# Weighing every second gathered row on VectorE instead of TensorE, with a ring of ten buffers

## The chip, the cores and the metric

The kernel runs on one core of one Trainium2 chip. The metric is the device time of one execution in microseconds (us). Before the change it is 3411.38 us, the median of three executions (3409.58 to 3421.29). The profile is of one further execution, whose own time was 3418.78 us.

## The reference, cut to what matters

Two transformer blocks run one after the other on 512 tokens of width 1024, all in float32. The first has a mixture-of-experts layer, the second ends in a layer that looks up single-neuron experts by product keys. The change is in that last layer alone:

```python
def peer_ffn(h, w_query, keys1, keys2, expert_u, expert_v):
    q = (hf @ w_query).reshape(t, PEER_HEADS, 2, PEER_HALF)        # 8 heads, 2 x 128
    s1 = jnp.einsum('thc,hnc->thn', q[:, :, 0], keys1)             # 128 keys each
    s2 = jnp.einsum('thc,hnc->thn', q[:, :, 1], keys2)
    ...                                                            # top 16 of 16 x 16 sums: idx, gate
    def block(args):
        hb, ib, gb = args
        act = jax.nn.gelu(jnp.einsum('thkd,td->thk', expert_u[ib], hb), approximate=False)
        return jnp.einsum('thk,thkd->td', gb * act, expert_v[ib])
```

Each token has 8 heads with 16 picks, 128 in all. For every pick a row `u` of 1024 and a row `v` of 1024 numbers are fetched; the dot product of `u` with the token goes through a gelu and times a gate becomes the pick's weight; the 128 rows `v` are summed with their weights. The block's output is that sum plus the residual, normalised by its root mean square.

## The kernel before, in words

The whole program is one launch in stages. The last stage is the function `peer`, which fills the last 40% of the execution. The 512 tokens lie in four tiles of 128, one token to a partition. The table `peer_uv` holds `u` and `v` of an expert side by side, 2048 numbers or 8 KB.

*Rows and ring.* A "row" in what follows is one indirect DMA of GpSimd (line 1833): for pick n of a tile it fetches 128 entries of `peer_uv`, one for each token, 1 MB in all, into slot n % RING of `ring`. RING is 11. There are 4 x 128 = 512 rows. GpSimd issues them in order; row n waits until row n - 11 is spent (line 1832).

*Batches and groups.* Two rows make a batch (256 batches), eight batches a group: the 16 picks of one head for one tile (32 groups). Groups alternate between tiles 0 and 1 for the first 16 groups, then between tiles 2 and 3.

*VectorE* runs in the order that the loop at line 2066 writes out: for batch b `products(b)` (two dot products of `u` with the token, line 2040, each behind the wait for its row), then `mixing(b - 1)` (weight = gelu times gate, two numbers for each token, line 2048). In the middle of every group, after batch 4 of 8, stands `retrieve(g + 2)` (lines 2005 to 2031): the top-16 search that finds the picks for the group after next. It runs for all groups but the last two, so 30 times in the loop. Before the loop stand `retrieve(0)` and `retrieve(1)`.

*ScalarE* computes the gelu of each batch (line 1941) and, in `diagonals`, for each row a 128x128 matrix with the weights on its diagonal (line 1948).

*TensorE* multiplies each row's diagonal matrix by the row's `v` half, in two calls of 512 columns that add into the tile's two PSUM banks (line 1907), and after each row raises `spent`. In float32 a call is two recorded passes, so a row has four. Between batches it also does what is left of the queries and scores for the first ten groups.

*End of a tile.* In groups 15, 16 and 31, at batches 2 and 3 of the group, ScalarE squares a finished tile's sum (`squares`, line 1956) and VectorE normalises it (`finish`, lines 2053 to 2058); the last tile is finished after the loop. SyncE stores it.

Of the kernel before, what the change touches and what calls it, by code (L numbers as in the profile page):

```python
# [18 lines left out]
ACT = mybir.ActivationFunctionType  # L19
ALU = mybir.AluOpType  # L20
AX = mybir.AxisListType

P = 128
D = 1024
# [4 lines left out]
NT = SEQ // P  # L29
# [18 lines left out]
HG_W = HG_H * HG_D  # L48
KH = HG_W // P
PEER_H, NKEYS, TOPK = 8, 128, 16  # L50
RING = 11
LEVELS = (32, 16, 8, 4, 2, 1)


# [1706 lines left out]
def peer(core, A, hn, out):  # L1761

    nc, ps, ident = core.nc, core.psum, core.ident
# [4 lines left out]
    DIAGS = 4  # L1768
    with core.stage("peer") as st:
# [14 lines left out]
        pick = st.sb("pick", [P, NT, PICKS], U32)  # L1784
        gate, dots = st.sb("gate", [P, NT, PICKS]), st.sb("dots", [P, NT, PICKS])
        acts, mix = st.sb("acts", [P, DIAGS, BATCH]), st.sb("mix", [P, DIAGS, BATCH])
        diag = st.sb("diag", [P, DIAGS, BATCH, P])
        stat = st.sb("stat", [P, NT, 4])
        hr = core.w.rows[:].rearrange("p (i b) c -> p i (b c)", b=2)
        gain = core.w.tiles[:, 0].rearrange("p k c -> p (k c)")  # L1790
        res = core.w.tiles[:, 1].rearrange("p k c -> p (k c)")
        (loaded, own, q_out, s_ps, s_out, r_ps, r_out, picked, e_in, e_out, dotted, gelued, mixed, diagonal, spent,
         squared, meaned, rooted, done, saved, gain_in) = (
            st.sem(n) for n in ("ld", "own", "qo", "sp", "so", "rp", "ro", "pick", "ei", "eo", "dot", "gelu", "mix",
                                "diag", "spent", "sq", "mean", "root", "done", "saved", "gain"))
        landed = [st.sem(f"row{n}") for n in range(RING)]
        w_ready, w_used, turns = core.w.ready, core.w.summed, core.w.turns

# [2 lines left out]

        def head_of(g):
            return g % (2 * H) // 2

        def place(b):
            g = b // PER
            return tile_of(g), head_of(g) * K + b % PER * BATCH

        with nc.Block() as block:
# [14 lines left out]
            @block.gpsimd  # L1824
            def _(pool):
                for n in range(NT * PICKS):
                    g, slot = n // K, n % RING
                    i, j = tile_of(g), head_of(g) * K + n % K
                    if n % K == 0:
                        pool.wait_ge(picked, g + 1)  # L1830
                    if n >= RING:
                        pool.wait_ge(spent, n - RING + 1)
                    pool.indirect_dma_start(out=ring[:, slot], out_offset=None, in_=A["peer_uv"],  # L1833
                                            in_offset=bass.IndirectOffsetOnAxis(ap=pick[:, i, j:j + 1], axis=0)
                                            ).then_inc(landed[slot], 16)

            @block.tensor
            def _(pe):
                def query(h, s):
                    m = 2 * h + s  # L1840
                    pe.wait_ge(w_ready[m % U], 16 * (turns + m // U + 1))
                    if h >= 1:
                        pe.wait_ge(q_out, 2 * (h - 1) + s + 1)
                    for k in range(KD):
                        last = nc.tensor.matmul(ps[:, 4 + s], core.w.tiles[:, m % U, k], hn[:, k], start=k == 0, stop=k == KD - 1)  # L1845
                    last.then_inc(w_used[m % U], 1)
# [19 lines left out]
                def residual(i):  # L1866
                    for k in range(KD):
                        nc.tensor.matmul(ps[:, 2 * i + k // 4, (k % 4) * P:(k % 4 + 1) * P],
                                         core.h[:, k, META + i * P:META + (i + 1) * P], ident[:],
                                         start=k % 4 == 0, stop=False, skip_group_check=True)  # L1870

                query(0, 0)
                query(0, 1)
                rows(0, 0)
# [11 lines left out]
                for b in range(BATCHES):  # L1886
                    i, j = place(b)
                    g, at = b // PER, b % PER
                    if g < 10 and at == 0:
                        query(3 + g // 2, g % 2)  # L1890
                    if g < 10 and g % 2 == 1 and at == PER // 2:
                        scores(3 + g // 2)
                    if g == 11 and at == 0:
                        pe.wait_ge(q_out, 2 * H)
                        rows(2, 4)
                    if g == 12 and at == 0:
                        pe.wait_ge(s_out, 2 * H)
                        rows(3, 6)
                    if g in (14, 15) and at == 0:
                        pe.wait_ge(r_out, 2 * NT)  # L1900
                        residual(g - 12)
                    pe.wait_ge(diagonal, BATCH * (b + 1))
                    for x in range(BATCH):
                        slot = (b * BATCH + x) % RING
                        end = j + x == PICKS - 1
                        for c in range(2):
                            last = nc.tensor.matmul(ps[:, 2 * i + c], diag[:, b % DIAGS, x], ring[:, slot, D + 512 * c:D + 512 * (c + 1)],  # L1907
                                                    start=False, stop=end, skip_group_check=True)
                        last.then_inc(spent, 1)

            @block.scalar
            def _(act):
# [30 lines left out]
                def diagonals(b):  # L1943
                    act.wait_ge(mixed, b + 1)
                    if b >= DIAGS:
                        act.wait_ge(spent, BATCH * (b - DIAGS + 1))
                    for x in range(BATCH):
                        act.activation(diag[:, b % DIAGS, x], ident[:], ACT.Copy, scale=mix[:, b % DIAGS, x:x + 1]).then_inc(diagonal, 1)  # L1948

                def squares(i):  # L1950
                    act.wait_ge(spent, PICKS * (2 * (i // 2) + 2) - (K if i % 2 == 0 else 0))
                    if i == 0:
                        act.wait_ge(gain_in, 16)
                    if i >= 1:
                        act.wait_ge(saved, 16 * i)
                    act.activation(res.rearrange("p (b c) -> p b c", b=2),
                                   ps[:, 2 * i:2 * i + 2], ACT.Square, accum_out=stat[:, i, 0:1]).then_inc(squared, 1)
                    act.wait_ge(meaned, i + 1)
                    act.activation(stat[:, i, 3:4], stat[:, i, 2:3], ACT.Sqrt).then_inc(rooted, 1)
# [33 lines left out]
            def _(dve):  # L1993
# [49 lines left out]
                def mixing(b):  # L2043
                    i, j = place(b)
                    dve.wait_ge(gelued, b + 1)
                    if b >= DIAGS:
                        dve.wait_ge(diagonal, BATCH * (b - DIAGS + 1))
                    dve.tensor_tensor(mix[:, b % DIAGS], acts[:, b % DIAGS], gate[:, i, j:j + BATCH],
                                      ALU.mult).then_inc(mixed, 1)

                def finish(i):
                    dve.wait_ge(squared, i + 1)
# [13 lines left out]
                for b in range(BATCHES):  # L2066
                    g, at = b // PER, b % PER
                    products(b)
                    if b >= 1:
                        mixing(b - 1)  # L2070
                    if at == PER // 2 and g + 2 < GROUPS:
                        retrieve(g + 2)
                    if g in (15, 16, 31) and at == 3:
                        finish({15: 0, 16: 1, 31: 2}[g])
                mixing(BATCHES - 1)
                finish(NT - 1)


# [129 lines left out]
```

## Time and profile before

| | |
|---|---|
| median of three executions | 3411.38 us (3409.58 to 3421.29) |
| the profiled execution's own time | 3418.78 us |
| its span | 3417.0 us |
| first and last issue of a row (line 1833) | 2043.6 and 3386.1 us |
| last dot product of a row starts (line 2040) | 3400.5 us |
| TensorE, VectorE, ScalarE, GpSimd busy over the span | 80%, 39%, 16%, 21% |
| mean granted clock of TensorE | 0.916 |

Times in the profile count from the start of the span. An engine is busy while an instruction of it executes; where it was idle, the profile names what released it. A row of a timeline gives start, duration and engine, then line, operation, output<-inputs and how many instructions were merged, and in brackets how long the engine sat idle before it and what ended that. VectorE is DVE, ScalarE is ACT, GpSimd is POOL and TensorE is PE there.

### The profile page before, as it was taken

Reading aid. Unit: us, or ns where it says so; the run is one execution under the profiler, and the core shown is the slowest. Engines: PE = TensorE matmul, PEld = TensorE weight load, DVE = VectorE, ACT = ScalarE, POOL = GpSimd, SP = SyncE. Lnnn points to the kernel's source line nnn. Section 1 sums busy time; section 2 is a strip of 40 time slices with the busy share of each in tenths; the row PEclk is TensorE's granted clock in tenths of the full one; section 3 lists DMA queues with packets and bytes.
Section 4 is the critical chain, followed back from the end, with each engine's and each line's share of the span. In section 5 each row is a group of like instructions: output and inputs, shape, how many; then the busy total and the mean of one; then the engine's idle time right before and its main releaser. Section 6 shows DMA issues by size and latency. Waiting matters only on the chain. (4 is left out here: it accounts for less than half of the span.)

```text
span 3417.0 us, 25695 instructions
## 1 busy us (share of the span) xinstructions
PE 2738.9 (80%) x9100; PEld 1266.1 (37%) x9100; DVE 1342.2 (39%) x3184; ACT 543.6 (16%) x1320; POOL 724.8 (21%) x624
## 2 busy tenths in 40 slices
PE   6999497777888787479899989888877777777777
PEld 4654333332333333234454444333433323323332
DVE  2151400000000000235320236767777777676674
ACT  2031100000000000021102012222222222222222
POOL 0000100000000000002420003444444444444442
PEclk9999699999999999689999999999988888888889
DMA  3003399999999999310112229999999999999998
GB/s 134 25 19 146 110 378 426 426 427 426 423 421 422 407 419 417 125 52 32 50 41 76 74 80 405 412 401 411 396 400 406 399 402 393 394 396 404 393 411 336
DMA packets 135119, 1017.95 MB, mean 298 GB/s; under 512 B 26624, under 2 KB 27344, under 8 KB 44368
## 3 DMA queue, kind: packets, MB, share of 16 engines
q0 software_dynamic: 83200, 545.33, 39.4%
q1 hardware_dynamic: 51792, 470.98, 33.8%
q8 instruction: 73, 1.20, 0.1%
q14 instruction: 54, 0.44, 0.0%
HBM read 1020.38 MB, written 21.02 MB: 305 GB/s over the span
## 5 line engine op out<-in xcount | busy, mean ns | idle before, releaser
L1907 PE MATMUL psum<-peer_ring,peer_diag 128*128 128x512 f32 x2048 | 970.1, 633 | 289.1 <-ACT peer_diag L1948 289.0
L1833 POOL DMA_INDIRECT peer_ring<-in_peer_uv,peer_pick x512 | 573.8, 1121 | 1063.5 <-PE psum L1907 739.3
L2040 DVE CUSTOM_DVE_ANT_0 peer_ring<-peer_ring,sb_rows 128x1024 f32<-128x1024 f32 x512 | 618.2, 1224 | 370.2 <-DMA peer_ring<-in_peer_uv,peer_pick 368.8
L1907 PEld LDWEIGHTS psum<-peer_ring,peer_diag 128*128 128x128 f32 x2048 | 408.4, 203 | 843.2 <-issue 483.2
L1089 PE MATMUL psum<-ffn1w_w,ffn_y 128*64 128x512 f32 x2048 | 487.4, 631 | 146.4 <-DMA ffn1w_w<-in_w_up 98.3
L1133 DVE TENSOR_TENSOR ffn_y<-psum,ffn_y 128x512 f32<-128x512 f32 x32 | 22.1, 692 | 883.7 <-ACT ffn_y L1117 883.7
L1089 PEld LDWEIGHTS psum<-ffn1w_w,ffn_y 128*64 128x64 f32 x2048 | 177.3, 145 | 455.2 <-issue 453.5
L1423 PE MATMUL psum<-mix_xn,sb_tiles 128*128 128x512 f32 x640 | 288.1, 612 | 14.7 <-DMA mix_heads<-in_head_pairs 14.7
L1110 PE MATMUL psum<-ffn1w_w,moe_hT 128*64 128x512 f32 x1024 | 230.0, 601 | 37.0 <-DVE moe_hT L1138 29.0
L1168 POOL DMA_INDIRECT expert_rows<-sb_tiles,ffn_block_tok x32 | 32.7, 1021 | 901.2 <-ACT sb_tiles L1123 874.7
L1941 ACT ACTIVATE peer_acts<-peer_dots 128x2 f32<-128x2 f32 x256 | 52.0, 203 | 880.1 <-DVE peer_dots L2040 880.0
L1423 PEld LDWEIGHTS psum<-mix_xn,sb_tiles 128*128 128x128 f32 x640 | 124.8, 197 | 171.5 <-issue 155.3
L1948 ACT ACTIVATE peer_diag<-sb_ident,peer_mix 128x128 f32<-128x128 f32 x512 | 173.5, 386 | 0.3
L1110 PEld LDWEIGHTS psum<-ffn1w_w,moe_hT 128*64 128x64 f32 x1024 | 85.3, 138 | 159.5 <-issue 159.5
L1845 PE MATMUL psum<-ffn_hn,sb_tiles 128*128 128x512 f32 x256 | 115.3, 604 | 11.4 <-PEq L144 10.5
L1117 ACT ACTIVATE ffn_y<-psum 128x512 f32<-128x512 f32 x32 | 19.1, 597 | 605.5 <-PE psum L1089 605.5
L412 PE MATMUL psum<-mix_xn,sb_tiles 128*128 128x264 f32 x384 | 91.5, 400 | 13.9 <-PEq L144 11.0
L1037 POOL DMA_INDIRECT slot_tokens<-ffn1r_tok,ffn_slots x8 | 8.0, 996 | 401.9 <-DVEq L1021 399.8
L1630 POOL TENSOR_TENSOR mix_K<-mix_z,mix_F 128x2048 f32<-128x2048 f32 x6 | 35.6, 5938 | 239.0 <-DVEq L1706 151.6
L412 PEld LDWEIGHTS psum<-mix_xn,sb_tiles 128*128 128x128 f32 x384 | 74.8, 197 | 29.9 <-issue 16.4
L1123 ACT ACTIVATE sb_tiles<-psum 128x512 f32<-128x512 f32 x64 | 34.7, 595 | 319.0 <-PE psum L1110 319.0
L1845 PEld LDWEIGHTS psum<-ffn_hn,sb_tiles 128*128 128x128 f32 x256 | 49.3, 194 | 73.8 <-issue 73.8
(351 smaller groups left out, 2112.1 us busy)
## 6 DMA issues: line engine op xcount, KB each, us to landing
ffn1w_w<-in_w_gate SPq DMA_DIRECT2D x64, 2048.0 KB, 28.9
ffn1w_w<-in_w_up SPq DMA_DIRECT2D x64, 2048.0 KB, 28.7
ffn1w_w<-in_w_down SPq DMA_DIRECT2D x64, 2048.0 KB, 29.9
sb_tiles<-in_w_in2b SPq DMA_DIRECT2D x28, 512.0 KB, 3.5
sb_tiles<-in_w_out SPq DMA_DIRECT2D x16, 512.0 KB, 3.5
sb_tiles<-in_w_query SPq DMA_DIRECT2D x16, 512.0 KB, 5.6
peer_ring<-in_peer_uv,peer_pick POOLq DMA_INDIRECT x512, 11.6
sb_tiles<-in_w_in SPq DMA_DIRECT2D x12, 512.0 KB, 3.5
```

Source lines behind the costliest of these rows:

```text
L412: last = nc.tensor.matmul(ps[:, bank(name) + half, 0:HALF], w_tile[:, n % U, k], xn[:, k, c], start=k == 0, stop=k == KD - 1)
L1089: last = nc.tensor.matmul(ps[r, bank], xT[:, u, k, r], weights(slots[half], k, F, 0, F), start=k == 0, stop=k == KD - 1)
L1110: last = nc.tensor.matmul(ps[r, 6 + b], hT[:, k, r], weights(slots[half], k, D, b * 512, 512), start=k == 0, stop=k == KE - 1)
L1123: act.activation(yo[:, u, b * 512:(b + 1) * 512], ps[:, 6 + b], ACT.Copy).then_inc(yo_ready, 1)
L1423: last = nc.tensor.matmul(ps[:, bank_of(n)], w_tile[:, n % U, c], xn[:, c], start=c == 0, stop=c == KD - 1)
L1630: pool.tensor_tensor(K[:, n % 2], k, F[:, n % 2], ALU.mult).then_inc(kl, 1)
L1833: pool.indirect_dma_start(out=ring[:, slot], out_offset=None, in_=A["peer_uv"], in_offset=bass.IndirectOffsetOnAxis(ap=pick[:, i, j:j + 1] ...
L1845: last = nc.tensor.matmul(ps[:, 4 + s], core.w.tiles[:, m % U, k], hn[:, k], start=k == 0, stop=k == KD - 1)
L1907: last = nc.tensor.matmul(ps[:, 2 * i + c], diag[:, b % DIAGS, x], ring[:, slot, D + 512 * c:D + 512 * (c + 1)], start=False, stop=end, sk ...
L1941: act.activation(acts[:, b % DIAGS], dots[:, i, j:j + BATCH], ACT.Gelu).then_inc(gelued, 1)
L1948: act.activation(diag[:, b % DIAGS, x], ident[:], ACT.Copy, scale=mix[:, b % DIAGS, x:x + 1]).then_inc(diagonal, 1)
L2040: dve.tensor_tensor_reduce(ring[:, n % RING, 0:D], ring[:, n % RING, 0:D], hr[:, i], 1.0, 0.0, ALU.mult, ALU.add, dots[:, i, j + x:j + x + ...
```

## The change

The first row of each batch goes the old way. The second row (odd n) is no longer given a diagonal matrix or multiplied on TensorE. VectorE multiplies its `v` half by the weight and adds it to a running sum of the tile in SBUF, `summed_rows`, in one instruction over 1024 columns; the first of a tile only multiplies. This is `weigh(b - 2)`, placed behind `mixing(b - 1)` and ahead of `retrieve`. When a tile is complete, TensorE adds its `summed_rows` to the tile's PSUM by two calls with the identity matrix (`fold`), and `squares` waits for that. The ring has ten slots, so that a slot always holds rows of the same parity; the issue of row n waits for `spent` or for `weighed` by that parity.

```diff
-RING = 11
+RING = 10
...
-        diag = st.sb("diag", [P, DIAGS, BATCH, P])
+        diag = st.sb("diag", [P, DIAGS, P])
+        summed_rows = st.sb("summed_rows", [P, 2, D])
...
+        def batches_of(i):
+            return NT * PICKS // BATCH // 2 * (i // 2 + 1) - (PER if i % 2 == 0 else 0)
...
                     if n >= RING:
-                        pool.wait_ge(spent, n - RING + 1)
+                        pool.wait_ge(weighed if (n - RING) % 2 else spent, (n - RING) // 2 + 1)
...
+                def fold(i):
+                    pe.wait_ge(weighed, batches_of(i))
+                    for c in range(2):
+                        last = nc.tensor.matmul(ps[:, 2 * i + c], ident[:], summed_rows[:, i % 2, 512 * c:512 * (c + 1)],
+                                                start=False, stop=True, skip_group_check=True)
+                    last.then_inc(folded, 1)
...
-                    pe.wait_ge(diagonal, BATCH * (b + 1))
-                    for x in range(BATCH):
-                        slot = (b * BATCH + x) % RING
-                        end = j + x == PICKS - 1
-                        for c in range(2):
-                            last = nc.tensor.matmul(ps[:, 2 * i + c], diag[:, b % DIAGS, x], ring[:, slot, D + 512 * c:D + 512 * (c + 1)],
-                                                    start=False, stop=end, skip_group_check=True)
-                        last.then_inc(spent, 1)
+                    pe.wait_ge(diagonal, b + 1)
+                    slot = b * BATCH % RING
+                    for c in range(2):
+                        last = nc.tensor.matmul(ps[:, 2 * i + c], diag[:, b % DIAGS], ring[:, slot, D + 512 * c:D + 512 * (c + 1)],
+                                                start=False, stop=False, skip_group_check=True)
+                    last.then_inc(spent, 1)
+                    if g in (15, 16, 31) and at == 1:
+                        fold({15: 0, 16: 1, 31: 2}[g])
+                fold(NT - 1)
...
                     if b >= DIAGS:
-                        act.wait_ge(spent, BATCH * (b - DIAGS + 1))
-                    for x in range(BATCH):
-                        act.activation(diag[:, b % DIAGS, x], ident[:], ACT.Copy, scale=mix[:, b % DIAGS, x:x + 1]).then_inc(diagonal, 1)
+                        act.wait_ge(spent, b - DIAGS + 1)
+                    act.activation(diag[:, b % DIAGS], ident[:], ACT.Copy, scale=mix[:, b % DIAGS, 0:1]).then_inc(diagonal, 1)
...
                 def squares(i):
-                    act.wait_ge(spent, PICKS * (2 * (i // 2) + 2) - (K if i % 2 == 0 else 0))
+                    act.wait_ge(folded, i + 1)
...
+                def weigh(b):
+                    i, j = place(b)
+                    row = ring[:, (b * BATCH + 1) % RING, D:2 * D]
+                    dve.wait_ge(mixed, b + 1)
+                    if j == 0:
+                        if i >= 2:
+                            dve.wait_ge(folded, i - 1)
+                        dve.tensor_scalar(summed_rows[:, i % 2], row, mix[:, b % DIAGS, 1:2], None, ALU.mult).then_inc(weighed, 1)
+                    else:
+                        dve.wait_ge(weighed, b)
+                        dve.scalar_tensor_tensor(out=summed_rows[:, i % 2], in0=row, scalar=mix[:, b % DIAGS, 1:2],
+                                                 in1=summed_rows[:, i % 2], op0=ALU.mult, op1=ALU.add).then_inc(weighed, 1)
...
                     products(b)
                     if b >= 1:
                         mixing(b - 1)
+                    if b >= 2:
+                        weigh(b - 2)
                     if at == PER // 2 and g + 2 < GROUPS:
                         retrieve(g + 2)
...
                 mixing(BATCHES - 1)
+                weigh(BATCHES - 2)
+                weigh(BATCHES - 1)
                 finish(NT - 1)
```

## Rows read from the trace of the kernel before

**Rows 1.** The page's second part: the span in 40 equal slices.
```profile
DMA  3003399999999999310112229999999999999998
GB/s 134 25 19 146 110 378 426 426 427 426 423 421 422 407 419 417 125 52 32 50 41 76 74 80 405 412 401 411 396 400 406 399 402 393 394 396 404 393 411 336
```
**Rows 2.** Stretch, length; busy PE, PEld, DVE, ACT, POOL; clock, DMA share, GB/s.
```profile
2056.00:3402.00 1346.00, 1055.96 (x2359) 456.68 (x2357) 931.58 (x2491) 314.60 (x931) 564.31 (x502) 0.90 0.99 402
```
**Rows 3.** Groups by line from 1900 us on.
```profile
L1907 PE MATMUL psum<-peer_ring,peer_diag 128*128 128x512 f32 x2048 | 970.1, 633 | 289.1 <-ACT peer_diag L1948 289.0
L2040 DVE CUSTOM_DVE_ANT_0 peer_ring<-peer_ring,sb_rows 128x1024 f32<-128x1024 f32 x512 | 618.2, 1224 | 370.2 <-DMA peer_ring<-in_peer_uv,peer_pick 368.8 <-DVE sb_tiles L2058 0.4
L1833 POOL DMA_INDIRECT peer_ring<-in_peer_uv,peer_pick x512 | 573.8, 1121 | 1063.5 <-PE psum L1907 739.3 <-DVE peer_pick L2028 293.9 <-issue 30.3
```
**Rows 4.** The chain of waits in order of time: the first and 30th such TensorE burst.
```profile
2094.05 15.19 PE psum L1907 x28
...
3318.76 20.69 PE psum L1907 x44
```
**Rows 5.** Timeline of VectorE around one retrieve.
```profile
2798.68 1.23 DVE L2040 CUSTOM_DVE_ANT_0 peer_ring<-peer_ring,sb_rows 128x1024 f32<-128x1024 f32 x1 [1.26 <-DMA peer_ring<-in_peer_uv,peer_pick]
...
2799.90 0.29 DVE L1999 MAX8 peer_val<-peer_far 128x8 f32<-128x128 f32 x1
...
2810.80 1.23 DVE L2040 CUSTOM_DVE_ANT_0 peer_ring<-peer_ring,sb_rows 128x1024 f32<-128x1024 f32 x1
...
2813.17 1.22 DVE L2040 CUSTOM_DVE_ANT_0 peer_ring<-peer_ring,sb_rows 128x1024 f32<-128x1024 f32 x1
...
2821.12 1.23 DVE L2040 CUSTOM_DVE_ANT_0 peer_ring<-peer_ring,sb_rows 128x1024 f32<-128x1024 f32 x1 [0.77 <-DMA peer_ring<-in_peer_uv,peer_pick]
2824.62 1.23 DVE L2040 CUSTOM_DVE_ANT_0 peer_ring<-peer_ring,sb_rows 128x1024 f32<-128x1024 f32 x1 [2.27 <-DMA peer_ring<-in_peer_uv,peer_pick]
...
2828.13 1.22 DVE L2040 CUSTOM_DVE_ANT_0 peer_ring<-peer_ring,sb_rows 128x1024 f32<-128x1024 f32 x1 [2.20 <-DMA peer_ring<-in_peer_uv,peer_pick]
...
2838.09 1.23 DVE L2040 CUSTOM_DVE_ANT_0 peer_ring<-peer_ring,sb_rows 128x1024 f32<-128x1024 f32 x1 [1.19 <-DMA peer_ring<-in_peer_uv,peer_pick]
2840.59 1.22 DVE L2040 CUSTOM_DVE_ANT_0 peer_ring<-peer_ring,sb_rows 128x1024 f32<-128x1024 f32 x1 [1.27 <-DMA peer_ring<-in_peer_uv,peer_pick]
```
**Rows 6.** Timeline of GpSimd and of TensorE around the same retrieve.
```profile
2804.76 0.94 POOL L1833 DMA_INDIRECT peer_ring<-in_peer_uv,peer_pick  x1 [0.78 <-PE psum L1907]
2818.11 1.82 POOL L1833 DMA_INDIRECT peer_ring<-in_peer_uv,peer_pick  x1 [12.41 <-PE psum L1907]
2821.02 0.94 POOL L1833 DMA_INDIRECT peer_ring<-in_peer_uv,peer_pick  x1 [1.09 <-PE psum L1907]
...
2814.06 16.13 PE L1907 MATMUL psum<-peer_ring,peer_diag 128*128 128x512 f32 x30 [9.57 <-ACT peer_diag L1948]
```
**Rows 7.** Timeline: an issue that starts just behind a dot product.
```profile
2663.96 1.23 DVE L2040 CUSTOM_DVE_ANT_0 peer_ring<-peer_ring,sb_rows 128x1024 f32<-128x1024 f32 x1 [1.26 <-DMA peer_ring<-in_peer_uv,peer_pick]
...
2664.03 1.96 POOL L1833 DMA_INDIRECT peer_ring<-in_peer_uv,peer_pick  x1 [0.53 <-PE psum L1907]
```
**Rows 8.** Groups by line, shapes apart: the same operation as the added one.
```profile
L171 DVE SCALAR_TENSOR_TENSOR ffn_hn<-sb_h,sb_vec,n_rs 128x512 f32<-128x512 f32 x8 | 5.4, 748 | 0.7 <-ACT n_rs L150 0.7
...
L1300 DVE SCALAR_TENSOR_TENSOR comb_g<-comb_g,ffn_gates 128x1024 f32<-128x1024 f32 x4 | 5.1, 1284 | 0.1
```
**Rows 9.** Timeline of ScalarE and VectorE where tile 1 is finished.
```profile
2703.47 1.00 ACT L1956 ACTIVATE sb_tiles<-psum 128x1024 f32<-128x1024 f32 x1
...
2708.38 1.41 DVE L2058 SCALAR_TENSOR_TENSOR sb_tiles<-psum,peer_stat,sb_tiles 128x512 f32<-128x512 f32 x2 [0.33 <-ACT peer_stat L1959]
...
2710.54 1.23 DVE L2040 CUSTOM_DVE_ANT_0 peer_ring<-peer_ring,sb_rows 128x1024 f32<-128x1024 f32 x1 [0.75 <-DMA peer_ring<-in_peer_uv,peer_pick]
```
**Rows 10.** Timeline of the end: the last dot product, and the last tile's squares.
```profile
3400.52 1.23 DVE L2040 CUSTOM_DVE_ANT_0 peer_ring<-peer_ring,sb_rows 128x1024 f32<-128x1024 f32 x1 [1.24 <-DMA peer_ring<-in_peer_uv,peer_pick]
...
3409.80 1.02 ACT L1956 ACTIVATE sb_tiles<-psum 128x1024 f32<-128x1024 f32 x1 [6.64 <-PE psum L1907]
```

More of the change, by code:

```diff
@@ L1791, in peer @@
         res = core.w.tiles[:, 1].rearrange("p k c -> p (k c)")
-        (loaded, own, q_out, s_ps, s_out, r_ps, r_out, picked, e_in, e_out, dotted, gelued, mixed, diagonal, spent,
+        (loaded, own, q_out, s_ps, s_out, r_ps, r_out, picked, e_in, e_out, dotted, gelued, mixed, diagonal, spent, weighed, folded,
          squared, meaned, rooted, done, saved, gain_in) = (
             st.sem(n) for n in ("ld", "own", "qo", "sp", "so", "rp", "ro", "pick", "ei", "eo", "dot", "gelu", "mix",
-                                "diag", "spent", "sq", "mean", "root", "done", "saved", "gain"))
+                                "diag", "spent", "weighed", "folded", "sq", "mean", "root", "done", "saved", "gain"))
         landed = [st.sem(f"row{n}") for n in range(RING)]
@@ L2046, in mixing @@
                     if b >= DIAGS:
-                        dve.wait_ge(diagonal, BATCH * (b - DIAGS + 1))
+                        dve.wait_ge(diagonal, b - DIAGS + 1)
                     dve.tensor_tensor(mix[:, b % DIAGS], acts[:, b % DIAGS], gate[:, i, j:j + BATCH],
                                       ALU.mult).then_inc(mixed, 1)
+                def weigh(b):
[10 more added lines that the diff above has]
+                                                 in1=summed_rows[:, i % 2], op0=ALU.mult, op1=ALU.add).then_inc(weighed, 1)
                 def finish(i):
```

## The prediction

> **What bounds the kernel now.** I read the page's slices first, to place the stage. In the last 17 slices, which are the gather stage, the DMA share stands at nine tenths or more, at 393 to 412 GB/s almost throughout [rows 1]. The view by stretches says it more sharply: from 2056 to 3402 us the DMA share is 0.99, while TensorE is busy 1056 of 1346 us, VectorE 932, GpSimd 564 and ScalarE 315 [rows 2]. Then the groups by line, for who waits for whom: VectorE sat idle 369 us before its dot products for the DMA of the row, TensorE 289 us for the diagonals behind them, and GpSimd 739 us for TensorE to free a slot [rows 3]. The last looks like a case against TensorE, but a ring behind a full queue is always full: that wait costs only what leaves the queue short of rows. So the stage is bound by the DMAs; 512 rows of 1.05 MB.
>
> The chain of waits has one burst of TensorE in each of the 30 groups that hold a `retrieve`; first and 30th begin 1224.7 us apart, so a group of 16 rows takes 1224.7/29 = 42.2 us [rows 4]. Undisturbed rows land 2.50 us apart (2838.09 to 2840.59), 40.0 us a group [rows 5]. The missing 2.2 us are lost after `retrieve`, and there the change acts. The timelines show it. Put t = 0 where the last dot product before it starts, at 2798.68. `retrieve` starts at 1.2 and occupies VectorE for 10.9; the next dot product starts at 12.1 [rows 5]. With 11 slots, nine rows are on order meanwhile: batches up to the one before are freed by TensorE early in the `retrieve`, the last by the issue at 2804.76 [rows 6]. The next batch's mixing must come before TensorE goes on: it restarts at 15.4, and its first row (late, after 9.6 us of idleness) frees a slot at 19.4 (2818.11), where GpSimd had waited 12.4 us [rows 6]. That issue takes 1.82 us, to 21.2, and its row lands at 25.9, 4.7 after the issue's end; the ninth had landed at 22.4. So 25.9 is 1.0 later than a full queue would give (24.9), and the row behind it comes 3.5 instead of 2.5 after it [rows 5, 6].
>
> **The change, part by part.**
>
> *Removed from TensorE and ScalarE:* half of 2048 passes (485 of 970 us busy) and 256 of 512 diagonals [rows 3]. Worth nothing by itself: both engines are covered by the DMAs. Four `fold`s add 16 passes, at most 10 us by the mean of 633 ns, covered but at the end. TensorE will be idle oftener; its half-rate start costs nothing as long as a row's 4 us [rows 6] fits in a batch's 5.
>
> *Added to VectorE:* 252 multiply-adds over 128x1024 from SBUF, and 4 plain multiplies. The trace has that very form once, at 1284 ns (two 512-wide ones would be 1496) [rows 8]. A dot product of 1224 ns [rows 3] follows the last after 1.15, so I take 1.21 us of pace, from 1.15 (nothing above a dot product) to 1.5 as bounds. A group of VectorE is now 8 x 2.37 (2810.80 to 2813.17) + 10.9 = 29.9 us [rows 5]; it becomes 29.9 + 8 x 1.21 = 39.5 of the 42.2. It still fits, but its slack falls from 12.3 us to 2.7.
>
> *Moved: when slots come free.* This is what I expect to decide. An odd row is freed only by `weigh(b - 2)`, one iteration later than the mixing, and `weigh` shares VectorE's queue with `retrieve`. At the start of `retrieve`, behind batch b, the weighs have got to b - 2. The odd row of batch b - 1 is thus held until the next iteration, and issues are in order. With ten slots, rows up to 2b + 8 are on order: seven instead of nine, 17.5 us of transfer instead of 22.5. One of the two lost rows is the ring's eleventh slot, the other the held odd row. The time line becomes: `weigh` 1.2, so `retrieve` from 2.4 to 13.3; two dot products and mixing to 15.7; `weigh(b - 1)` to 17.0; GpSimd some 0.3 later at 17.3. That is 2.1 earlier than the 19.4 of now, since it doesn't wait for TensorE.
>
> *The issue itself.* The next dot product has just started by then, and issues that start behind one are long: 1.96 us when it had begun 0.07 earlier, 0.94 when free [rows 6, 7]. So it ends at 19.1 and the row lands at 19.1 + 4.7 = 23.8. That is the row that a full queue gives at 8 x 2.5 = 20.0. The gap grows from 1.0 to 3.8 us, so +2.8 for each `retrieve`.
>
> On this the Trainium skill has a rule (SBUF — State Buffer, "Who interferes with whom"): a VectorE instruction with two SBUF inputs contends with a GpSimd instruction that reads SBUF, and the one that issued first keeps the shared port. The 1.96 us issue agrees. The added instruction is of that sort too, so by this rule it also speaks against the change; without it the issue would take 0.94 and the sum would be some 27 us smaller.
>
> *A shallow queue after the gap.* Today most issues behind the gap are short, and the queue refills as fast as TensorE frees slots. Then they fall where VectorE runs two-input instructions without a break, so each may take up to 1.96 us [rows 7] and the pause between two, hardly less than the 2.5 in which a row lands. The row after a gap takes 3.5 instead of 2.5 today [rows 5]; up to two more may do so. Bounds 0 to +1.8 a group; I take +0.4, near the lower end, since VectorE frees slots in backlog at 3.6 us for two.
>
> *Sum for a `retrieve`:* +2.8 + 0.4 = +3.2 us. Bounds: +1.9 with a short issue; +4.6 with the whole shallow-queue loss; a pace of 1.15 or 1.5 changes two weighs, -0.1 or +0.6. Thirty times: 96 us (54 to 156).
>
> *Beginning.* Before the loop's first `retrieve` the first weighs are themselves in backlog: +2.8 once.
>
> *Finishing tiles.* `squares` of tiles 0 and 1 had nothing to wait for at 2703.47; VectorE's normalising then ended at 2709.8, 0.8 before the next row was in [rows 9]. It will wait for a batch's row and the fold, eight passes: 4.3 us at 28 passes in 15.19 [rows 4], 8 at the slow start's 4.05 a row. Between the squares' end at 2704.5 and the normalising at 2708.38 lie 3.9 us, and 0.8 behind it, so a later `retrieve` costs 0 to 3.3 us, twice; I take 3 in all.
>
> *End.* Now 9.3 us pass from the last dot product (3400.52) to the last squares (3409.80), mostly TensorE's last rows [rows 10]. Then: dot product 1.2, three weighs 3.6, fold 2.2 to 4, so 7.0 to 8.8. Gain 0.5 to 2.3; I take 2, since TensorE has had half the rows.
>
> *Total:* 96 + 3 + 3 - 2 = +100 us. On the profiled execution's own 3418.8 us (span 3417.0) that is 3519; that execution lies 7.4 above the median, so I forecast 3411 + 100 = **3511 us**.
>
> **The rivals.**
>
> *Faster: the late restart was the loss.* GpSimd's long wait after `retrieve` is for TensorE, and the change frees every other slot without it. Were seven rows on order enough to bridge the earlier restart, the 2.2 us lost in each group would vanish: 30 x -2.2 = -66, and 3411 - 66 + 4 = 3349 us. For it: the restart is 2.1 earlier, and the slow first rows of TensorE are off half the slots. Against: the lost cover is 5.0 us. It decides only if rows issued at 17.3 land before 20, in 2.7 us, where the trace's fastest issue to landing was 6.3.
>
> *No change: the transfers hide it anyway.* The 5.0 us lost and 2.1 won come out even if the present loss is mostly not the ring's but of the chip's memory. Today some landings are late with rows on order. If such a loss took up the gap, the time would be 3411 + 4 = 3415. Against: the landing at 25.9 follows its issue by the usual 4.7.
>
> *VectorE becomes the bound.* Its group reaches the forecast's 45.4 us when a weigh costs 1.9, and if an issue that starts first held up VectorE for 0.94, sixteen times a group, it would be 39.5 + 15 = 54.5: +12.3 x 30, 3780 us. A weigh of 2.4 (twice a dot product) gives 29.9 + 19.6 = 49.5, +7.3 a group, 3630 us. Against: issues at 2818.11 ran beside dot products that kept their 1.15 us.
>
> By the skill's rule above the hold-up can go that way as well; no row here shows VectorE's pace broken.
>
> **How the numbers follow.** The forecast has 76%, and of itself runs from 3411 + 54 + 0 = 3465 to 3411 + 156 + 8 = 3575. VectorE as the bound has 7% (3575 up), no change 7%, faster 10%. The range is 3440 to 3590: the forecast's own with the neighbourhood of both edges; some 2 in 10 lie outside. A measurement of this kernel tells 0.5%, 17 us, from no change. Slower by more: 76 + 7 = 83%; within: 7%; faster: 10%.
>
> **What would show it.** Right: in the trace after, GpSimd's first issue after `retrieve` released by VectorE's weigh at about 17.3 and long; its row at 23.8 and eighth in line, with seven dot products without a wait before it; a group of 45.4 us; DMA share of the stage down to about 0.92; VectorE busy some 88%; multiply-adds of 1.28 us. Wrong in size: several rows 3.5 apart after the gap. Wrong altogether: groups of 40 to 42 us with the share at 0.99, or VectorE without waits for rows at all.

## Result: 2.4% slower, and the profile after

The change makes the kernel slower: 3500.5 us in the median of four executions (3497.5 to 3504.5) against 3416.3 us of the kernel before (four executions on the same chip). The ratio is 1.0242, with a 95% interval of 1.0216 to 1.0268. The forecast was 3511 us, with a range of 3440 to 3590; 3500.5 lies 10 below it. Part of that nearness is luck: as an increase the forecast said +100 us and the medians say +84, and 5 of the 16 us between them are made up by a kernel before that took 3416.3 us here and 3411.4 in the executions the forecast started from.

The same views as before. First the stretch of the gather stage (length; busy time of the engines; granted clock, DMA share, GB/s), which answers to [rows 2], then the groups by line that answer to [rows 3] and [rows 8] (from 2043 us on, so without the first eight issues).

```profile
2056.00:3480.00 1424.00, 749.61 (x1327) 274.96 (x1326) 1219.14 (x2734) 238.05 (x671) 652.39 (x502) 0.77 0.92 376
```

```profile
L1916 PE MATMUL psum<-peer_ring,peer_diag 128*128 128x512 f32 x1024 | 663.7, 791 | 675.9 <-ACT peer_diag L1959 675.8
L1837 POOL DMA_INDIRECT peer_ring<-in_peer_uv,peer_pick x504 | 654.3, 1298 | 773.8 <-DVE peer_summed_rows L2072 439.2 <-PE psum L1916 224.7 <-issue 104.6
L2051 DVE CUSTOM_DVE_ANT_0 peer_ring<-peer_ring,sb_rows 128x1024 f32<-128x1024 f32 x512 | 615.1, 1222 | 164.4 <-DMA peer_ring<-in_peer_uv,peer_pick 162.2 <-DVE sb_tiles L2082 0.6
L2072 DVE SCALAR_TENSOR_TENSOR peer_summed_rows<-peer_ring,peer_mix,peer_summed_rows 128x1024 f32<-128x1024 f32 x252 | 322.0, 1278 | 0.1
```

The DMA share of the stage fell from 0.99 to 0.92, the figure that the forecast named. VectorE is busy 1219 of 1424 us, 86% (some 88% in the forecast). TensorE lost half its passes but only 306 of 970 us of busy time: the mean pass grew from 633 to 791 ns, since its granted clock fell from 0.90 to 0.77 of 2.4 GHz over the stage. It now waits for the diagonals before most batches, 676 us in all. The multiply-add takes 1278 ns.

Then one `retrieve` of the kernel after, first on VectorE, then on GpSimd and TensorE. It answers to [rows 5, 6]; t = 0 is again the start of the last dot product ahead of it, 2842.46.

```profile
2842.46 1.23 DVE L2051 CUSTOM_DVE_ANT_0 peer_ring<-peer_ring,sb_rows 128x1024 f32<-128x1024 f32 x1 [1.27 <-DMA peer_ring<-in_peer_uv,peer_pick]
...
2843.68 1.28 DVE L2072 SCALAR_TENSOR_TENSOR peer_summed_rows<-peer_ring,peer_mix,peer_summed_rows 128x1024 f32<-128x1024 f32 x1
...
2855.78 1.23 DVE L2051 CUSTOM_DVE_ANT_0 peer_ring<-peer_ring,sb_rows 128x1024 f32<-128x1024 f32 x1
...
2858.15 1.28 DVE L2072 SCALAR_TENSOR_TENSOR peer_summed_rows<-peer_ring,peer_mix,peer_summed_rows 128x1024 f32<-128x1024 f32 x1
2859.35 1.22 DVE L2051 CUSTOM_DVE_ANT_0 peer_ring<-peer_ring,sb_rows 128x1024 f32<-128x1024 f32 x1
...
2871.17 1.22 DVE L2051 CUSTOM_DVE_ANT_0 peer_ring<-peer_ring,sb_rows 128x1024 f32<-128x1024 f32 x1
...
2874.42 1.23 DVE L2051 CUSTOM_DVE_ANT_0 peer_ring<-peer_ring,sb_rows 128x1024 f32<-128x1024 f32 x1 [0.76 <-DMA peer_ring<-in_peer_uv,peer_pick]
```

```profile
2859.70 1.68 POOL L1837 DMA_INDIRECT peer_ring<-in_peer_uv,peer_pick  x1 [11.73 <-DVE peer_summed_rows L2072]
2862.80 1.00 POOL L1837 DMA_INDIRECT peer_ring<-in_peer_uv,peer_pick  x1 [1.42 <-PE psum L1916]
2864.11 1.97 POOL L1837 DMA_INDIRECT peer_ring<-in_peer_uv,peer_pick  x1 [0.30 <-issue]
2866.39 0.97 POOL L1837 DMA_INDIRECT peer_ring<-in_peer_uv,peer_pick  x1 [0.30 <-issue]
...
2858.75 6.09 PE L1916 MATMUL psum<-peer_ring,peer_diag 128*128 128x512 f32 x8 [12.49 <-ACT peer_diag L1959]
```

Weigh at 1.2, next dot product at 13.3, `weigh(b - 1)` from 15.7, and GpSimd released by it at 17.2 with a long issue (1.68 us) to 18.9: each within 0.2 us of the forecast's time line. The release stands at 17.2 in 28 of the 30 groups. One thing is different. VectorE doesn't come to wait for the row issued then. It has so much work that it runs ten dot products without a wait, to 2871.17; only the eleventh, at 32.0, waits for its row. The first dot products that show the empty queue come three rows later than I wrote.

That the queue does stand empty can be read from the DMA engines. These are the four emptiest microseconds around the `retrieve` shown, in the kernel after (15.5 to 19.5 us behind t = 0) and, below, in the kernel before (19.3 to 23.3). The columns are those of [rows 2]; the DMA share is the last but one:

```profile
2858.00:2862.00 4.00, 3.25 (x4) 1.17 (x4) 4.00 (x10) 0.74 (x4) 1.68 (x1) 0.50 0.15 61
2818.00:2822.00 4.00, 4.00 (x8) 1.56 (x7) 3.23 (x6) 1.52 (x6) 2.75 (x2) 0.74 0.42 107
```

The trace also has the semaphore updates with which a row's parts are reported, 16 for a row; the row has landed with the last of them. Over the 27 groups in which no tile is finished, the eighth row lands 23.4 us behind t = 0 in the median (forecast 23.8) and 5.9 behind the seventh. With a full queue it is 2.5, and in the kernel before the tenth row lands 3.2 behind the ninth. So the gap stands where the forecast put it and has nearly its size.

### The profile page after: what moved, and what is told of

Read it like the earlier page. It is cut to its first block and busy times, and to the rows that moved or that the text cites. A ratio compares the mean times of both kernels' runs of the same rounds, so it can differ in the third digit from the quotient of the medians.

```text
span 3495.7 us, 23933 instructions
## 1 busy us (share of the span) xinstructions
PE 2444.0 (70%) x8092; PEld 1089.2 (31%) x8092; DVE 1638.2 (47%) x3440; ACT 469.1 (13%) x1064; POOL 812.9 (23%) x624
## 5 line engine op out<-in xcount | busy, mean ns | idle before, releaser
L1916 PE MATMUL psum<-peer_ring,peer_diag 128*128 128x512 f32 x1024 | 663.7, 791 | 675.9 <-ACT peer_diag L1959 675.8
L1837 POOL DMA_INDIRECT peer_ring<-in_peer_uv,peer_pick x512 | 661.9, 1293 | 1069.8 <-DVE peer_summed_rows L2072 439.2
L1089 PE MATMUL psum<-ffn1w_w,ffn_y 128*64 128x512 f32 x2048 | 496.9, 642 | 134.4 <-DMA ffn1w_w<-in_w_up 99.0
L1916 PEld LDWEIGHTS psum<-peer_ring,peer_diag 128*128 128x128 f32 x1024 | 224.4, 241 | 1102.9 <-ACT peer_diag L1959 914.9
L2072 DVE SCALAR_TENSOR_TENSOR peer_summed_rows<-peer_ring,peer_mix,peer_summed_rows 128x1024 f32<-128x1024 f32 x252 | 322.0, 1278 | 0.1
L1959 ACT ACTIVATE peer_diag<-sb_ident,peer_mix 128x128 f32<-128x128 f32 x256 | 98.8, 386 | 1.0 <-DVE peer_mix L2059 0.8
```

The lines of the kernel that those rows point to most:

```text
L1089: last = nc.tensor.matmul(ps[r, bank], xT[:, u, k, r], weights(slots[half], k, F, 0, F), start=k == 0, stop=k == KD - 1)
L1916: last = nc.tensor.matmul(ps[:, 2 * i + c], diag[:, b % DIAGS], ring[:, slot, D + 512 * c:D + 512 * (c + 1)], start=False, stop=False, ski ...
L1959: act.activation(diag[:, b % DIAGS], ident[:], ACT.Copy, scale=mix[:, b % DIAGS, 0:1]).then_inc(diagonal, 1)
L2072: dve.scalar_tensor_tensor(out=summed_rows[:, i % 2], in0=row, scalar=mix[:, b % DIAGS, 1:2], in1=summed_rows[:, i % 2], op0=ALU.mult, op1 ...
```

## Experiments

All are read by the same measure beside their time: the mean length of a group of 16 rows over 29 groups, from the start of the tenth dot product of each group to that of the next group's. It is 42.24 us before and 45.20 after.

### 1. The eleventh slot alone

```diff
--- the kernel before
-RING = 11
+RING = 10
```

> The kernel before with a ring of ten slots instead of eleven, nothing else. Theory (what counts is how many rows are on order while retrieve occupies VectorE, against when the first slot comes free behind it): eight rows on order instead of nine, restart unchanged at 19.4, so the row issued then still lands at 25.9 but is the ninth, not the tenth: +2.5 us in each of 30 groups, +75 us, 3416 to 3491 us, group 44.7 us. Rival (the slot is not scarce, VectorE's added work or the odd row's late release is the whole loss): under +10 us.

Measured: 3490.2 us, ratio to before 1.0213 (1.0191 to 1.0234), group 44.89 us. One slot less costs 2.65 us a group, nearly all that the whole change does. Its timelines:

```profile
2836.75 1.23 DVE L2040 CUSTOM_DVE_ANT_0 peer_ring<-peer_ring,sb_rows 128x1024 f32<-128x1024 f32 x1 [1.26 <-DMA peer_ring<-in_peer_uv,peer_pick]
...
2857.11 1.22 DVE L2040 CUSTOM_DVE_ANT_0 peer_ring<-peer_ring,sb_rows 128x1024 f32<-128x1024 f32 x1
2862.59 1.22 DVE L2040 CUSTOM_DVE_ANT_0 peer_ring<-peer_ring,sb_rows 128x1024 f32<-128x1024 f32 x1 [4.18 <-DMA peer_ring<-in_peer_uv,peer_pick]
...
2842.92 0.93 POOL L1833 DMA_INDIRECT peer_ring<-in_peer_uv,peer_pick  x1 [0.31 <-PE psum L1907]
2856.02 1.98 POOL L1833 DMA_INDIRECT peer_ring<-in_peer_uv,peer_pick  x1 [12.17 <-PE psum L1907]
```

The release is where it was (19.3), the row issued then lands at 25.8 as before, but it is the ninth and not the tenth: VectorE waits 4.2 us for it. The rival is out.

### 2. VectorE's added instruction alone

The kernel before, ring of eleven, with a multiply-add of the same shape at the same place; it reads the token's row and leads nowhere. (`sc2`, `cand2` and `hit` share a buffer to make room.)

```diff
+                    dve.scalar_tensor_tensor(out=spare_sum[:], in0=hr[:, i], scalar=mix[:, b % DIAGS, 1:2],
+                                             in1=spare_sum[:], op0=ALU.mult, op1=ALU.add).then_inc(weighed, 1)
...
                         mixing(b - 1)
+                    if b >= 2:
+                        weigh(b - 2)
```

> The kernel before (ring of eleven, all rows on TensorE) with the added multiply-add of VectorE at the same place in its order, but reading the token's row instead of the gathered one and leading nowhere: VectorE's time and port use alone (two scratch tiles share a buffer to make room). Theory: retrieve starts 1.2 us later and with it the mixing that restarts TensorE: +1.2 us a group, +36 us, some 3452 us, no more since 39.5 us of VectorE still fit in a group. Rival (VectorE's load or its hold on GpSimd's issues is the loss): +85 us or more, 3500.

Measured: 3451.8 us, 1.0098 (1.0074 to 1.0123), group 43.28 us, +1.04. The slot that TensorE frees behind `retrieve` comes free at 20.6 instead of 19.4 in the trace, and that is all: VectorE's 39.5 us fit. The rival is out.

### 3. The kernel after with eleven slots

```diff
--- the kernel after
-RING = 10
+RING = 11
```

(With the shared buffer and `KEPT`, the number of score tiles held, 3 instead of 4, since the eleventh slot and the 8 KB of sums don't fit otherwise.)

> The kernel after with a ring of eleven (two scratch tiles share a buffer and one kept score tile less, to make room). Theory: eight rows on order instead of seven during retrieve, release at 17.3 unchanged: -2.5 us a group, about -75 us, 3425 us, group 42.2. Rival (VectorE's own order is what paces the group now): under -20 us, above 3480.

Measured: 3420.4 us, 1.0008 (0.9996 to 1.0020) to the kernel before, group 42.40 us. The slot takes back 2.80 of the 2.96 us that the change cost. With eleven slots each the two kernels are the same within measurement. `KEPT` 3 was not run by itself; the first six groups are longer than in the kernel before (43.6 against 42.6 us in the mean) and the other 23 are not (42.1 against 42.2).

### 4. The odd row free one iteration sooner

```diff
--- the kernel after
-                    if b >= 2:
-                        weigh(b - 2)
+                    if b >= 1:
+                        weigh(b - 1)
```

> The kernel after, with each weigh directly behind its own batch's mixing instead of one iteration later, ring of ten. The odd row of batch b-1 is free before retrieve, so eight rows are on order instead of seven. Theory: the next row then waits for TensorE's even row of batch b, whose mixing comes at 15.7 and whose slow first passes end at about 19.9; with its issue it lands at about 26.4, where the same row lands in the kernel after anyway. So within 15 us of 3500. Rival (the held odd row is one of the two that are missing and costs its 2.5 us): 3425 us.

Measured: 3519.6 us, 1.0304 (1.0282 to 1.0326), group 45.52 us: 19 us slower than the kernel after, 4 outside what I expected, and on the other side from the rival. VectorE and GpSimd behind a `retrieve` (t = 0 at 2855.55):

```profile
2869.00 1.23 DVE L2051 CUSTOM_DVE_ANT_0 peer_ring<-peer_ring,sb_rows 128x1024 f32<-128x1024 f32 x1
2870.15 1.22 DVE L2051 CUSTOM_DVE_ANT_0 peer_ring<-peer_ring,sb_rows 128x1024 f32<-128x1024 f32 x1
2871.49 1.28 DVE L2072 SCALAR_TENSOR_TENSOR peer_summed_rows<-peer_ring,peer_mix,peer_summed_rows 128x1024 f32<-128x1024 f32 x1
2872.69 1.22 DVE L2051 CUSTOM_DVE_ANT_0 peer_ring<-peer_ring,sb_rows 128x1024 f32<-128x1024 f32 x1
...
2875.63 1.64 POOL L1837 DMA_INDIRECT peer_ring<-in_peer_uv,peer_pick  x1 [11.64 <-PE psum L1916]
2877.57 1.98 POOL L1837 DMA_INDIRECT peer_ring<-in_peer_uv,peer_pick  x1 [0.30 <-issue]
```

There is now one row more on order (+2.5 us of cover), but the first release is TensorE's even row, at 20.1 here and 20.45 in most groups, 3.2 later than the weigh's 17.2. The row issued then is the ninth, and it lands at 26.3 in the median; the ninth row of the kernel after, one behind its gap, lands at 26.0. So the theory held, and the row held by the lag was no loss that comes back by freeing it: the next slot in order is TensorE's, and it comes no sooner. A batch in backlog also takes 3.69 us instead of 3.56, as the weigh must wait for the mixing right ahead of it. Only part of the 19 us is the gather stage's: from the first issue to the end of the span it is 9.9 us longer than in the kernel after (0.32 a group), and between the two profiled executions, 17.8 us apart, the other 7.9 lie ahead of the stage, where the code is the same.

### 5 to 7. `retrieve` in three parts

```diff
-                def retrieve(g):
+                def search(g):          # top 16 of both halves
...
+                def combine(g):         # top 16 of the sums, up to e_in
...
+                def pick_rows(g):       # the rest
...
-                    if at == PER // 2 and g + 2 < GROUPS:
-                        retrieve(g + 2)
+                    if at in (2, 4, 6) and g + 2 < GROUPS:
+                        (search, combine, pick_rows)[at // 2 - 1](g + 2)
```

The kernel before with it:

> The kernel before, with retrieve cut into three parts (3.4, 3.1 and 4.3 us) behind batches 2, 4 and 6 of the group instead of one of 10.9 behind batch 4. Theory: nine rows on order outlast every part, so the 2.2 us lost in each group go: group 40.0 to 40.3, -55 to -66 us, 3355 us. Rival (the 2.2 us are the memory's own late landings): within 10 us of 3417.

The kernel after with it:

> The kernel after with the same cut, ring of ten. Theory: the gap behind retrieve goes here too, and what remains is VectorE's 39.5 us a group against 40.0 of transfers: group 40.0 to 41.5, 3360 to 3405 us, DMA share of the stage 0.97 or more. Rival (so little slack makes VectorE the bound, with its long issues): above 3430.

The kernel before with it and ten slots:

> The kernel before with the cut and a ring of ten. Theory: the eleventh slot was worth 75 us only because of the long retrieve; with short parts it is worth under 10 us: 3355 to 3365 us. Rival (a slot is worth 2.5 us a group whatever VectorE's order): 3430.

| `retrieve` in three parts | us | ratio to before | group, us | one piece |
|---|---|---|---|---|
| before, 11 slots | 3377.0 | 0.9899 (0.9882 to 0.9915) | 40.89 | 42.24 |
| before, 10 slots | 3383.1 | 0.9909 (0.9892 to 0.9925) | 41.08 | 44.89 |
| after, 10 slots | 3383.7 | 0.9916 (0.9899 to 0.9932) | 41.09 | 45.20 |

Both kernels before are some 20 us above what I expected, the kernel after is in its range. The slot that was worth 73 us is worth 6, within the intervals. The change, which cost 84 us as it was made, costs 7, hardly more than can be told. So the long `retrieve` is what makes slots count. The kernel before with the cut beats both kernels of this study, by 1.0% and 3.5%. Its timeline around the first part, and the stretch from 2100 to 3300 us of it:

```profile
2798.84 1.23 DVE L2050 CUSTOM_DVE_ANT_0 peer_ring<-peer_ring,sb_rows 128x1024 f32<-128x1024 f32 x1 [1.26 <-DMA peer_ring<-in_peer_uv,peer_pick]
2800.06 0.29 DVE L1999 MAX8 peer_val<-peer_far 128x8 f32<-128x128 f32 x1
...
2803.46 1.22 DVE L2050 CUSTOM_DVE_ANT_0 peer_ring<-peer_ring,sb_rows 128x1024 f32<-128x1024 f32 x1
2804.61 1.22 DVE L2050 CUSTOM_DVE_ANT_0 peer_ring<-peer_ring,sb_rows 128x1024 f32<-128x1024 f32 x1
2806.32 1.23 DVE L2050 CUSTOM_DVE_ANT_0 peer_ring<-peer_ring,sb_rows 128x1024 f32<-128x1024 f32 x1 [0.41 <-DMA peer_ring<-in_peer_uv,peer_pick]
```

```profile
2100.00:3300.00 1200.00, 972.43 (x2147) 405.83 (x2146) 872.12 (x2342) 287.41 (x854) 538.32 (x470) 0.95 1.01 416
```

Two rows of backlog, and the third finds VectorE waiting for it again. The share is 1.01, so the queue doesn't run dry, and yet a group takes 40.9 us in the mean, not the 40.0 that I had set as the floor. The first six groups, in which TensorE also has queries and scores to do, take 41.6; the later ones mostly 39.9 or 40.9. The timeline of VectorE shows what makes the difference, in four dot products of which each had to wait for its row:

```profile
3032.55 1.22 DVE L2050 CUSTOM_DVE_ANT_0 peer_ring<-peer_ring,sb_rows 128x1024 f32<-128x1024 f32 x1 [0.76 <-DMA peer_ring<-in_peer_uv,peer_pick]
3035.04 1.23 DVE L2050 CUSTOM_DVE_ANT_0 peer_ring<-peer_ring,sb_rows 128x1024 f32<-128x1024 f32 x1 [1.19 <-DMA peer_ring<-in_peer_uv,peer_pick]
3038.49 1.23 DVE L2050 CUSTOM_DVE_ANT_0 peer_ring<-peer_ring,sb_rows 128x1024 f32<-128x1024 f32 x1 [2.22 <-DMA peer_ring<-in_peer_uv,peer_pick]
3040.99 1.22 DVE L2050 CUSTOM_DVE_ANT_0 peer_ring<-peer_ring,sb_rows 128x1024 f32<-128x1024 f32 x1 [1.19 <-DMA peer_ring<-in_peer_uv,peer_pick]
```

One row comes 3.45 us behind the last instead of 2.5. By the semaphore updates this happens about once in 22 rows from the eighth group on, once in 18 to 21 in the kernel after with the cut, and few rows are late otherwise; once in 22 makes 0.7 us a group. What delays that row isn't shown. The theory had the mechanism and 20 us too much of it.

### 8. Relief of TensorE alone

```diff
--- the kernel before
-                        for c in range(2):
+                        wide = 512 if x == 0 or end else 64
+                        for c in range(2 if wide == 512 else 1):
```

> The kernel before (ring of eleven), with TensorE's work on odd rows cut to 64 of their 1024 columns (the sum lacks the others), VectorE's order and the slots' release unchanged: the relief of TensorE alone. Theory (TensorE is covered by the transfers, and the slot that counts behind retrieve is an even row's): within 10 us of 3414. Rival (TensorE's slow passes behind retrieve cost the group part of its 2.2 us): -20 to -40 us.

Measured: 3413.4 us, 1.0000 (0.9985 to 1.0014), group 42.39 us. Nearly half of TensorE's work in the stage is worth nothing, though TensorE was busy 1056 of 1346 us of it (786 of 1339 now) and GpSimd waited 739 us for it. One thing this run can't tell: the row that frees the first slot behind `retrieve` is an even one, which it leaves whole, and its slot still comes free at 19.4. Experiment 2 shows that this moment counts: 1.2 us later cost 1.04 us a group. A TensorE faster there was not tried.

### 9. The same time on VectorE with one input from SBUF

```diff
--- the kernel of experiment 2
-                    dve.scalar_tensor_tensor(out=spare_sum[:], in0=hr[:, i], ..., in1=spare_sum[:], op0=ALU.mult, op1=ALU.add)
+                    dve.tensor_reduce(spare_sum[:], hr[:, i], AX.X, ALU.add)
```

> The kernel extra_op with the added multiply-add replaced by a sum over the token's row, an instruction of nearly the same length that reads one SBUF tensor instead of two. Theory by this case's rows (an issue that starts behind a two-input instruction waits for its end): issues behind the sum take 0.94 us again, mean issue down from 1.254 to about 1.12 us; the time follows only where the first issue behind retrieve gets shorter, 0 to 0.9 us a group: 3452 down to 3425 at most. Rival (issue length plays no part in the 1.2 us a group): within 5 us of 3452.

Measured: 3446.3 us, 1.0089 (1.0066 to 1.0112), group 43.16 us; mean issue 1.162 us against 1.254 with the multiply-add. First an issue behind the multiply-add of experiment 2, then one behind the sum:

```profile
2405.99 1.28 DVE L2060 SCALAR_TENSOR_TENSOR peer_spare_sum<-sb_rows,peer_mix,peer_spare_sum 128x1024 f32<-128x1024 f32 x1
...
2406.09 1.99 POOL L1835 DMA_INDIRECT peer_ring<-in_peer_uv,peer_pick  x1 [0.43 <-PE psum L1909]
```

```profile
2444.69 1.21 DVE L2057 TENSOR_REDUCE peer_spare_sum<-sb_rows 128x1 f32<-128x1024 f32 x1
...
2445.00 0.94 POOL L1835 DMA_INDIRECT peer_ring<-in_peer_uv,peer_pick  x1 [0.65 <-PE psum L1909]
```

Counted over the stage, the issues that start with 0.5 us or more of the other instruction still to run: 42 behind the multiply-add take 1.66 us in the mean, 62 behind the sum 0.94, as much as with VectorE idle. What holds an issue is the second input from SBUF. Here the Trainium skill (SBUF — State Buffer, "Who interferes with whom") says just this, and the trace agrees. In time it is little: the two kernels' intervals overlap, and the 5.5 us between them can't be told from nothing, so neither theory nor rival is decided.

### 10. Finishing a tile behind `retrieve`

```diff
--- the kernel after, on ScalarE and on VectorE
-                    if g in (15, 16, 31) and at == 2:      # squares
+                    if g in (15, 16, 31) and at == 5:
...
-                    if g in (15, 16, 31) and at == 3:      # finish
+                    if g in (15, 16, 31) and at == 6:
```

> The kernel after with squares and finish of tiles 0, 1 and 2 three batches later (5 and 6 of the group, behind retrieve instead of just ahead of it). Theory: the two groups of 48.7 and 48.0 us in its trace come down to 44 to 46, -5 to -8 us in all, 3493 us. Rival (the fold itself costs it): groups of 48 stay, 3500.

Measured: 3498.7 us, 1.0235 (1.0210 to 1.0261). The two groups of 48.7 and 48.0 us, with the one behind them at 44.4, became 44.8, 46.5 and 46.3: 3.5 us less, and a part moved to the next group. The whole stage is 6.4 us shorter in this trace than in that of the kernel after, as expected, but the medians differ by 1.8 us, within the scatter of single executions (3492.4 to 3501.4). So whether the gain is real stays open.

### 11. The kernel after with both, three parts and eleven slots

```diff
--- the kernel after of experiment 3, and the diff of experiments 5 to 7
```

> The kernel after with retrieve in three parts and a ring of eleven (room made as in after_ring11). With the transfers at 40.9 us a group and VectorE at 39.5, theory: the slot is worth 0 to 10 us more, 3375 to 3384, no better than the kernel before with the cut (3377). Rival (odd rows still come free too late): 3365 or less, and better than the kernel before with the cut.

Measured: 3380.4 us, 0.9897 (0.9874 to 0.9921), group 41.03 us. No better than the kernel before with the cut; odd rows come free soon enough once no long `retrieve` stands in their way.

## Why the prediction was right

*The direction and the mechanism* were right: the stage is bound by its transfers, and the change leaves them short of rows on order behind each `retrieve`. Experiment 3 gives the slot back and has the old time; experiments 5 to 7 take away the long occupation of VectorE, and neither slot nor change matters much.

*Two rows of cover against an earlier restart.* The forecast set 5.0 us lost against 2.1 won. Both show: release at 17.2 instead of 19.4 in the trace, the slot's 2.65 us in experiment 1. The second lost row, the odd one held by the lag, costs as much as the first on paper, but experiment 4 shows that it and the earlier release belong together: without the lag both go, and the time gets no better. Going from experiment 1 (44.89) to the kernel after (45.20), all of VectorE's new work and order nets 0.31 us a group. So the loss of the change as it was made is nearly all the eleventh slot's.

*Terms of the sum*, in us, from the two traces:

| term | forecast | measured |
|---|---|---|
| for a `retrieve` | +3.2 (1.9 to 4.6 by the bounds) | +2.76 |
| beginning, up to the first group's middle | +2.8 | +0.4 |
| two groups with a finished tile, beyond that | +3 | +5.8 |
| end, last dot product to end of span | -2 | -0.5 |
| whole stage | +100 | +90 |

The measured terms, with 30 times the first, make 88.5 us; the 1.4 us left fall behind the 30th `retrieve`, where tile 2 is finished. The first measured figure is the mean over the 27 groups without a finished tile: (29 x 45.20 - 48.7 - 48.0)/27 = 44.97 against (29 x 42.24 - 44.1 - 41.3)/27 = 42.21, so 2.76. By the landings both parts of the forecast's term are there. The gap itself grew by 2.6 us in the median and 2.9 in the mean (forecast 2.8); the four rows behind it took 0.3 longer in the mean than the four behind the gap of the kernel before (forecast 0.4); the other rows of the group took 0.3 less, for which the forecast had no term. The row behind the gap comes 2.7 us after it in the mean (3.2 in the kernel before), and no string of rows 3.5 apart follows. The stage from first issue to the end of the span went from 1373.4 to 1463.3 us, +90. The spans differ by less, 78.7, since the stages ahead of it, which have the same code, took 11.2 us less in the profiled execution of the kernel after. The medians differ by 84.

*Finishing tiles.* This term was too small. The squares wait for eight TensorE passes at a granted clock of 0.55, which stands in the last row below as the first of its three closing numbers; ahead of them TensorE had been idle for 4.02 us:

```profile
2744.64 1.02 ACT L1967 ACTIVATE sb_tiles<-psum 128x1024 f32<-128x1024 f32 x1 [6.81 <-PE psum L1879]
...
2737.89 3.78 PE L1916 MATMUL psum<-peer_ring,peer_diag 128*128 128x512 f32 x4 [4.02 <-ACT peer_diag L1959]
2741.47 3.14 PE L1879 MATMUL psum<-peer_summed_rows,sb_ident 128*128 128x512 f32 x4
...
2737.80:2744.70 6.90, 6.72 (x8) 2.52 (x8) 4.50 (x7) 0.09 (x2) 3.77 (x3) 0.55 1.02 426
```

That is 6.8 us of waiting, inside the 4.3 to 8 that I gave; but what stands behind the squares is late too, which I left out: the next batch's dot products had ended at 2742.3, and its gelu ran at 2748.58, behind the squares and the root that the normalising needs. That this makes the rest of the term is argued; no run isolates it.

*A step that was wrong in part:* "the missing 2.2 us are lost after `retrieve`". With the cut the share is 1.01 and a group still takes 40.9 us. So `retrieve` in one piece made 1.35 of the 2.2 us (42.24 to 40.89). Some 0.9 stays when the queue no longer runs dry: 0.7 of it is the one late landing in about 22 rows of experiments 5 to 7, the rest lies in the first six groups. The sum did not rest on it, since it compared two time lines. A slip on which nothing rests either: the gather stage fills the last 16 slices of [rows 1] and not 17, and the last of them has a share of eight tenths at 336 GB/s.

*The rivals.* "Faster" and "no change" fell with the 0.92. Their argument, that the earlier release wins, holds only as far as it pays for the held odd row and VectorE's new work: with equal slots the change still costs 0.2 to 0.3 us a group (42.24 to 42.40 with eleven, 44.89 to 45.20 with ten). With eleven the times are the same within the measurement; with ten the medians are 10 us apart and the single executions don't overlap (3489.1 to 3494.4 against 3497.5 to 3504.5), so a small loss is likely there. "VectorE becomes the bound" is out too: dot products keep their 1.15 us pace beside long issues, and experiment 3 runs groups of 42.4 us with the same work on VectorE.

## What to carry to other kernels

Where one engine both frees buffers and has a long uninterrupted job, count for the moment when that job starts: how many transfers are on order, how long they last, and when the first release behind the job comes. Here the change of time was the change of that difference, and the engines' busy shares didn't tell of it. And before adding buffers or moving work off the engine that seems to be waited for, cut the long job into parts: here this won 1.0% where taking away nearly half of TensorE's work won nothing, and it made the eleventh buffer all but superfluous.

## What the runs showed of the hardware

- An indirect DMA's issue on GpSimd takes 0.94 us, and waits for the end of a VectorE instruction with two inputs from SBUF that had started first; one with a single SBUF input doesn't hold it (42 issues at 1.66 us, 62 at 0.94). Back-to-back instructions of the first sort on VectorE don't lock it out: it gets in between two, and they keep their pace. In the kernel after the issue of 2859.70 ends at 2861.38, beside dot products that start at 2859.35 and, 1.14 us later, at 2860.49.
- A row of 1.05 MB lands 4.5 to 4.7 us after the end of its issue with the queue empty (means of the first row behind the gap, kernel after and experiment 1), and 2.5 us behind the row before with the queue full. By the Trainium skill (DMA: Bandwidth & Descriptors, "Anatomy of one DMA", the fit of a fixed 2.0 us plus bytes over 436 GB/s) it would be an estimated 4.4, and the traces are near that.
- With the queue never empty (experiments 5 to 7), rows landed 2.5 us apart but for about one in 20 that came 3.45 us behind the last, so that groups of 16 took mostly 39.9 or 40.9 us. What causes it was not tested.
- TensorE's passes got longer as its work was halved: 633 to 791 ns, with a granted clock of 0.77. A row's four passes take 1.98 us at full clock; after the pause of 4.02 us at 2737.89 they took 3.78, with a granted clock of 0.55 over them and the fold, near the lower of the two levels.
